# PSUM banks given out by the list scheduler, and a scheduler model with transfer issue time and a shared port: a hybrid conformer and sliding-window layer on eight cores

## What is computed

```python
def reference(x, ...):
    x = x + 0.5 * swiglu_ffn(rmsnorm(x, ffn1_norm), ffn1_w_in, ffn1_w_out)   # hidden width 2816
    h = rmsnorm(x, mix_norm)
    u_conv, q, k, v, g_conv, g_attn = split(h @ w_in)        # 2048, 1024, 256, 256, 1024, 1024
    a = conformer_conv(u_conv, ...)   # GLU, causal depthwise conv of width 31, layer norm, SiLU, projection
    b = sliding_window_gqa(q, k, v, ...)   # 16 q heads, 4 kv heads, window 128, QK norm, T5 bias, sinks
    x = x + (sigmoid(g_conv) * a + sigmoid(g_attn) * b) @ w_out
    return x + 0.5 * swiglu_ffn(rmsnorm(x, ffn2_norm), ffn2_w_in, ffn2_w_out)
```

## Time and profile before

| | us |
|---|---|
| runs of the kernel (median of 3) | 3554.66 (3302.78 to 3849.4) |
| profiled execution: time | 3302.84 |
| profiled execution: span of the slowest core (the profile is of this core) | 3301.1 |
| spans of the eight cores | 3278.3 to 3301.1 |
| TensorE busy (93% of the span) | 3071.1 |
| VectorE, ScalarE, GpSimd busy | 1557.6, 938.3, 779.6 |

### The profile page before, as it was taken

One profiled execution on the slowest core, in us unless ns is written; L12 is line 12 of the kernel. 1 busy time (PEld: TensorE's weight loads), 2 busy tenths in 40 slices (PEclk: granted clock), 3 DMA queues, 4 the chain that ended last, 5 costly groups with the idle time before them and its releaser, 6 DMA issues.

```text
span 3301.1 us, 43930 instructions; the slowest of 8 cores (3278.3 to 3301.1 us)
## 1 busy us (share of the span) xinstructions
PE 3071.1 (93%) x15348; PEld 1402.3 (42%) x15348; DVE 1557.6 (47%) x2374; ACT 938.3 (28%) x1447; POOL 779.6 (24%) x542
## 2 busy tenths in 40 slices
PE   3999999999998999997789999999699999999998
PEld 1444444444443545554333333333244444444444
DVE  5444457544465546364344343344464445533444
ACT  3111135211132232323764444443221112311110
POOL 2100012000012523425165544446200000100000
PEclk9999999999999999998899999999899999999999
DMA  6422236422263432426354334446612223522212
GB/s 166 77 37 38 42 108 167 90 39 39 39 156 114 135 100 85 139 63 175 106 117 141 122 122 122 125 112 213 167 33 38 39 46 104 133 39 39 39 20 102
DMA packets 146772, 312.38 MB, mean 95 GB/s; under 512 B 48896, under 2 KB 57088, under 8 KB 142464
## 3 DMA queue, kind: packets, MB, share of 16 engines
q1 hardware_dynamic: 115744, 221.84, 21.4%
q0 software_dynamic: 30816, 87.74, 16.0%
HBM read 288.19 MB, written 100.66 MB: 118 GB/s over the span
## 4 chain that ended last, share of the span: by engine, by line
PE 79%; DVE 5%; DMA 5%; issue 4%; ACT 3%; SPq 2%; POOL 1%; DVEq 0%; ACTq 0%; POOLq 0%
PE ps L363 79%; SPq L391 2%; DMA xA_45<-x 1%; DVE zfm L618 1%; DVE y L674 1%; DMA xA_43<-x 1%; DMA zsh<-zfm 1%; ACT et_163 L377 0%; DMA xC_182<-x 0%; DMA sg_161<-sig_s 0%; DVE hA_49 L438 0%; POOL toep_92 L643 0%; DVE hA_48 L438 0%; DMA xA_44<-x 0%; POOL toep_90 L643 0%
## 5 line engine op out<-in xcount | busy, mean ns | idle before, releaser
L652 DVE TENSOR_TENSOR y<-ps,cbias 128x512 f32<-128x512 f32 x64 | 43.9, 690 | 185.1 <-PE ps L363 140.5
L377 ACT ACTIVATE tfC_210<-ps 128x512 f32<-128x512 f32 x44 | 26.3, 597 | 311.1 <-PE ps L363 311.1
L377 ACT ACTIVATE tfA_73<-ps 128x512 f32<-128x512 f32 x44 | 26.2, 596 | 286.6 <-PE ps L363 286.5
L377 ACT ACTIVATE et_163<-ps 128x1024 bf16<-128x1024 f32 x63 | 64.3, 1021 | 109.4 <-PE ps L363 108.8
L755 POOL TENSOR_TENSOR pt_166<-et_162,EB 128x1024 bf16<-128x1024 bf16 x31 | 66.3, 2139 | 109.3 <-ACT et_162 L377 109.1
L377 ACT ACTIVATE et_162<-ps 128x1024 bf16<-128x1024 f32 x63 | 64.2, 1018 | 78.1 <-PE ps L363 77.9
L377 ACT ACT_TABLE_LOAD x52 | 66.7, 1283 | 68.1 <-PE ps L363 58.2
L755 POOL TENSOR_TENSOR pt_165<-et_163,EB 128x1024 bf16<-128x1024 bf16 x32 | 68.4, 2138 | 10.8 <-ACT et_163 L377 9.1
L755 POOL TENSOR_TENSOR pt_164<-et_162,EB 128x1024 bf16<-128x1024 bf16 x32 | 68.4, 2138 | 7.9 <-ACT et_162 L377 7.2
L508 DVE SCALAR_TENSOR_TENSOR xA_45<-ps,xA_45 128x512 f32<-128x512 f32 x96 | 64.8, 689 | 11.3 <-PE ps L363 10.6
L508 DVE SCALAR_TENSOR_TENSOR xC_183<-ps,xC_183 128x512 f32<-128x512 f32 x96 | 64.9, 690 | 10.8 <-PE ps L363 9.9
(11 more groups left out here) (747 smaller groups left out, 7440.3 us busy)
## 6 DMA issues: line engine op xcount, KB each, us to landing
zsh<-zfm SPq DMA_DIRECT2D x256, 32.0 KB, 2.0
hM<-h SPq DMA_DIRECT2D x8, 1024.0 KB, 6.9
cact<-cact_s SPq DMA_DIRECT2D x8, 1024.0 KB, 5.8
sig_s<-tfB_124 SPq DMA_DIRECT2D x24, 256.0 KB, 2.3
sig_s<-tfB_125 SPq DMA_DIRECT2D x24, 256.0 KB, 2.3
cact_s<-ct_126 SPq DMA_DIRECT2D x6, 1024.0 KB, 7.2
sg_156<-sig_s SPq DMA_DIRECT2D x22, 256.0 KB, 3.6
sg_157<-sig_s SPq DMA_DIRECT2D x22, 256.0 KB, 4.3
```

Source lines behind the costliest of these rows:

```text
L377: P.add("act", lambda e: e.activation(**kw), reads, writes, 0.21 + n / 1200.0 + (0.3 if accum is not None else 0.0), table=TABLE.get(func))
L652: dve(lambda e, b=b, yv=yv, G=G: e.tensor_tensor(out=yv.ap, in0=ps[:, b, :].rearrange("p (g r c) -> p g r c", g=4, r=8), in1=cbias.t[:, 64 ...
```

## The change

The device work is the same; the bank of each matmul, the order of the queues and the semaphore waits that follow from it are not.

- A bank is now an object (`Bank`) with a list of spots it may take: `ANY` (7 down to 0; SwiGLU, norm and convolution), `MIX` (7 down to 2; q, k, v, the two accumulators, merge, output projection) and `TWO` (the pairs 0, 1 and 2, 3; scores). The first operation that uses it allocates it when the scheduler puts that operation into TensorE's queue. It is given back when its last user has been scheduled, free in model time 0.3 us after the last reader's end.
- `place` looks for spots that no live bank holds and takes the first in the list that is free by then. Projections of q and k are marked `hold`: at most three of them live at once.
- TensorE's step looks at the first 64 ready matmul groups in list order (`SCAN`), asks `place` for each, and takes the first among those that can start earliest (`PATIENCE` 0).
- Model costs: a transfer on SP occupies its queue for 0.64 us up to 64 KB and 0.45 us above (0.1 before). An operation of GpSimd, and one of VectorE with two larger inputs in SBUF (`two`), each wait until the other's is over. Results reach TensorE 0.3 us and other engines 0.12 us after their end (0.2 before). One small GpSimd operation costs 1.7 instead of 0.6.

The diff, cut to its core:

```diff
+SCAN = 64
+PATIENCE = 0.0
+class Bank:
+    def __init__(self, spots, hold=False):
+        self.spots, self.hold = spots, hold
+        self.ops = []
+        self.i = None
...
+    def place(self, o, t):
+        taken, spots = set(), []
+        for b in o.alloc:
+            if b.hold and self.held >= 3:
+                return None, None
+            best = None
+            for sp in b.spots:
+                if any(self.owner[x] is not None or x in taken for x in sp):
+                    continue
+                at = max(self.bfree[x] for x in sp)
+                if best is None or max(at, t) < max(best[0], t):
+                    best = (at, sp)
+            if best is None:
+                return None, None
+            t = max(t, best[0])
+            taken.update(best[1])
+            spots.append(best[1])
+        return t, spots
...
+                if e == "pe":
+                    cand = []
+                    for i in pe_new[:SCAN]:
+                        at, spots = self.place(ops[i], max(free[e], ready[i]))
+                        if at is not None:
+                            cand.append((at, i, spots))
+                    if not cand:
+                        continue
+                    low = min(c[0] for c in cand)
+                    t = low
...
+            if e == "pe":
+                t, pick, spots = next(c for c in cand if c[0] <= low + PATIENCE)
+                pe_new.remove(pick)
+                o = ops[pick]
+                for b, sp in zip(o.alloc, spots):
+                    b.i = sp[0]
+                    b.at = sp
+                    self.held += b.hold
+                    for x in sp:
+                        o.deps.update(self.bprev[x])
+                        self.owner[x] = b
...
+            if o.dma is None and (e == "pool" or o.two):
+                t = max(t, lock["dve" if e == "pool" else "pool"])
+                lock[e] = t + cost
...
+            for b in o.banks:
+                mm_left[b] -= 1
+                if not mm_left[b]:
+                    self.held -= b.hold
+                    for x in b.at:
+                        self.owner[x] = None
+                        self.bfree[x] = max(ops[i].end + (0.3 if ops[i].eng != "pe" else 0.0) for i in b.ops)
+                        self.bprev[x] = b.ops
             for s in succ[pick]:
-                lat = 0.0 if (ops[s].eng == e and o.dma is None) else 0.2
+                lat = 0.0 if (ops[s].eng == e and o.dma is None) else 0.3 if ops[s].eng == "pe" else 0.12
...
+    ANY = [(i,) for i in range(7, -1, -1)]
+    MIX = [(i,) for i in (7, 6, 5, 4, 3, 2)]
+    TWO = [(0, 1), (2, 3)]
...
-        return P.add(eng, fn, reads, writes, 0.1 if q == "sp" else 1.0, dma=key, nbytes=nbytes, after=after)
+        return P.add(eng, fn, reads, writes, (0.64 if nbytes <= 65536 else 0.45) if q == "sp" else 1.0, dma=key, nbytes=nbytes, after=after)
...
-        b = 7
+        b = Bank(ANY)
...
-                ba, bb = banks7.next(), banks7.next()
+                ba, bb = Bank(ANY), Bank(ANY)
...
-    bankB, bankC, bankL = Ring([0, 1, 2, 3, 4]), Ring([5, 6]), Ring([7])
...
-    bankM, bankS, bankV = Ring([0, 1, 2, 3]), Ring([(4, 5)]), Ring([(6, 7)])
...
-            b = bankM.next()
+            b = Bank(MIX, True)
...
-            bo, bd = bankV.next()
+            bo, bd = Bank(MIX), Bank(MIX)
...
-                b0, b1 = bankS.next()
+                sb = Bank(TWO)
```

More of the change, by code:

```diff
@@ L1 @@
+import bisect
 import heapq
@@ L61 @@
 class Op:
-    __slots__ = ("eng", "fn", "deps", "cost", "table", "dma", "nbytes", "start", "end", "pos", "val", "raw", "i")
+    __slots__ = ("eng", "fn", "deps", "cost", "table", "dma", "nbytes", "start", "end", "pos", "val", "raw", "i",
+                 "two", "banks", "alloc")
 class Prog:
@@ L74, in __init__, with add @@
         self.last_dma = {}
-    def add(self, eng, fn, reads, writes, cost, table=None, dma=None, nbytes=0, after=()):
+    def add(self, eng, fn, reads, writes, cost, table=None, dma=None, nbytes=0, after=(), two=False):
         o = Op()
+        o.two, o.banks, o.alloc = two, [], []
         o.i = len(self.ops)
@@ L110, in add @@
             self.last_dma[dma] = o.i
+        for v in list(reads) + list(writes):
+            b = getattr(v, "bank", None)
+            if b is not None and b not in o.banks:
+                o.banks.append(b)
+                if not b.ops:
+                    o.alloc.append(b)
+                b.ops.append(o.i)
         deps.discard(o.i)
@@ L455, in ffn @@
         last = [None]
-        banks7.n = 0 if first else 4
         def load_x(t):
```

175 lines of the change are left out of this document (96 added, 79 removed).

## The result

Two executions of the changed kernel took 3208.29 and 3217.18 us, beside 3300.71 and 3302.78 of the kernel before: a ratio of 0.973, with a 95% interval of 0.967 to 0.979. A second, later measurement gave 0.974 (0.972 to 0.976; 3214.74 and 3216.47 us). The kernel is faster by 2.7%.

The account below looks back on a forecast made before the run. TensorE was taken as the bound, its idle time mostly waits for PSUM banks, which also lower the clock. Bank gains of 71 us, minus 6 for bank choice, plus 5 for costs, gave 70 us: 3233 us, range 3175 to 3320.

Parts of the forecast that it names:

- A: Whole kernel: bank waits were the cause and 60% comes back; 3233 us, own range 3205 to 3265, chance 0.50.
- within: Whole kernel: time not told from no change, about 2% either way, between 3237 and 3369 us; chance 0.48.
- What stays: at nothing, since no edit reaches them: Start (58 us), full SwiGLU slices and second SwiGLU's start (32 us between 2300 and 2400): no gain.
- the loss of 6 for the bank choice: SwiGLU: taking the first free bank in the list, not the longest free, loses slack behind late readers; 6 us.
- Attention, 40 us: Attention, merge, output projection (1700 to 2300 us): three quarters of 54 us of bank waits and their clock come back.
- the announced 25 us: Attention: sign of being right, TensorE's idle time falls from 44 to under 25 us.
- Hand-over and convolution, 19 + 12 by banks and 5 by costs: 1041 to 1700 us: banks gain 19 of 42 us in hand-over, 12 of 22 in convolution; both model edits 5.
- the bound of 10.1 us on both cost edits: Matmuls behind toep: SP issue time and port model together gain between 0 and 10.1 us; half taken.
- The announced signs: Convolution: ct waits go from 12.3 to under 3 us; toep waits halve.
- B: Hand-over and attention: data waits replace bank waits, idle time stays behind pt, sq, toep; 3283 us, chance 0.22.
- C: SwiGLU, norms of late tiles: reusing the latest freed bank makes TensorE wait behind late readers; 3330 us, chance 0.14.
- D: Whole kernel: all bank and toep waits go, with their clock, 128 us; 3175 us, chance 0.14.

Follow-up runs that it names:

- the run with the late start: Changed kernel with the second tile's norm matmul kept ahead of the first tiles' SwiGLU matmuls, which then start near 50 us: 3194.02 us, ratio 0.967.

## Why the prediction failed, and what of it was right

The time was 3208 to 3217 us where 3233 was forecast, inside the range of 3175 to 3320 and inside A's own. A was the mechanism. What failed is the forecast itself: no change beyond 2% was held the likeliest, "within" at 0.48 against "faster" at 0.45, and the kernel is 2.7% faster. The sum of 70 us, 4 us past the bound of 2%, was too small. The step that failed is "What stays: at nothing, since no edit reaches them". On a core at full clock the stages held at nothing gave 32 us of the 44 that were missing, attention 8 more, and the loss of 6 for the bank choice stands in no stage's balance (convolution and hand-over: 2 less than forecast). On the slowest cores themselves (core 5 before, core 7 after: 94 us) attention gave 14 more than forecast and the last stage 12; the first stage's gain went there into the clock of 0.81. Term by term:

- **Attention, 40 us: undersized.** It gave 48 to 51 (644.2 to 596.1 or 592.9; rings put back: 648.1). Three quarters of 54 was too careful: with no engine above 52% beside TensorE, most bank waits went, and their clock with them. Releasers afterwards in the window of the earlier trace rows, in their order:

```profile
PE ps L470 <- POOL mg L893: 12.4, 1, 12.4
PE ps L470 <- DVE xC_181 L607: 4.9, 1, 4.9
PE ps L470 <- DVE tfM_170 L863: 3.8, 4, 1.0
PE ps L470 <- ACT et_163 L478: 2.1, 4, 0.5
```

  The two largest lie behind the last score, which now comes inside the window: mg is the operand of the last tile's output projection, xC belongs to the second SwiGLU. Without them 14.7 of the 32.0 us are left. So by the fixed window the announced 25 us were missed, and up to the last score they were kept; the clock is the announced 0.98, and o and qn are gone from the list.
- **Hand-over and convolution, 19 + 12 by banks and 5 by costs: right in sum (36 against 34), wrong in cause.** Banks alone took 8 where 31 were forecast, since the waits for a bank came back behind the tanh (29.3 us); the costs alone took 29 where 5 were. The failing step there is the bound of 10.1 us on both cost edits, taken from the waits for toep. It priced only what the model says about those instructions. With the costs alone TensorE waits less for qn, too (3.1 us on core 5, 9.9 before). The announced signs came: ct at 1.3 us in the convolution (12.3 before), no wait for toep.

```profile
PE ps L470 <- ACT ct_126 L478: 1.3, 5, 0.4
```

  From 1500 to 1700 us, ct_127 still takes 7.6 us on core 7, and one late zsh 14.6: data, as the prediction had it for a part of that stage.

```profile
PE ps L470 <- DMA zsh<-zfm: 14.6, 1, 14.6
PE ps L470 <- ACT ct_127 L478: 7.6, 6, 2.7
```

- **What stays, at 0: the failed step.** First and last stage gave 21 and 11 us on a core at full clock. "No edit reaches them" was wrong: the rings of SwiGLU and the norm go as well, and an order that changes in the stage behind changes what runs at the seam. The stretch before the first zsh, on core 5 before and after (columns of the earlier trace rows), has lost its idle time:

```profile
940.00:1041.00 101.00, 91.00 (x413) 40.32 (x411) 77.15 (x126) 37.23 (x58) 26.69 (x23) 0.98 0.68 173
```

```profile
940.00:1016.00 76.00, 76.00 (x353) 34.34 (x352) 58.67 (x114) 36.36 (x55) 14.82 (x15) 1.00 0.73 191
```

  Up to 150 us the same core is busy for 105.4 us where it was for 95.0: the early start, of which little is left at the end of the stage, as the run with the late start shows. At the start of the second SwiGLU, TensorE's waits before (2280 to 2420 us, core 5; columns as in the earlier trace rows) and after (2197 to 2337, core 7) are:

```profile
PE ps L363 <- DVE hC_186 L438: 11.2, 1, 11.2
PE ps L363 <- DVE hlC_221 L432: 10.5, 1, 10.5
PE ps L363 <- DVE hC_187 L438: 8.4, 1, 8.4
```

```profile
PE ps L470 <- POOL mg L893: 12.4, 1, 12.4
PE ps L470 <- DVE xC_181 L607: 4.9, 1, 4.9
PE ps L470 <- DVE hidC_193 L595: 2.0, 1, 2.0
```

  Before, the first SwiGLU groups stood ahead of the last tile's output projection in the queue, and TensorE waited three times for a tile's norm. After, the whole output projection comes first; it waits once for its operand mg, and no wait for a norm is left. Which part of the change brings that order stays open, since several runs with banks on demand lose the gain again.

- **Bank choice, 6 us of loss: right in size, wrong in place.** The longest-free choice gains 4 us by the stages and 8 by the time (late start, 3194.02 to 3186.08), and it gains them in the convolution, behind the tanh, not in SwiGLU. There TensorE is idle from 531 to 990 us for 0.9 to 2.1 us on those four cores at full clock, behind hid and x; the 8.1 us are those of core 7, which had been at 0.81.
- **Not foreseen: the clock of 0.81**, 25 us on the slowest cores. It hid about a fifth of the gain. That 3233 lay so near is luck: the sum of 70 us was too small by 44, and this loss was missing.
- **Rivals.** B is out: in attention the idle time went and was not replaced. The Trainium skill's page "TensorE: Matmul & The Clock Gate", section "HAM oscillation — how this bites in real kernels", reports no further gain from PSUM double-buffering in a kernel reworked because its gaps came from transfers; here the gaps came from the banks, and freer banks gave 48 us. C is out in SwiGLU beyond a few us, but its mechanism, a bank taken behind a late reader, is what the banks alone met in the convolution. D's 3175 is near the spans of the cores at full clock (3160 to 3187), and to the best kernel's 3186, but not by D's way: waits for a bank are left (26.7 us of idle time in attention, 15.9 us behind tfB), and the first and last stage make up for them.

## To carry to other kernels

A wait for a PSUM bank on a nearly full TensorE is worth its length and, here, over half as much again in granted clock, and in attention, where the other engines are half idle, most of it came back. A bank given out on demand can also bring a wait, when its last reader is late for reasons of its own: look at who reads the bank before, and what that engine waits for. A planner's cost is no local term: one number that is nearer to the chip moved the queues of the whole stage, so it is priced by the idle time of the whole stage and not by the waits of the instruction that it describes, and leaving it out of the finished kernel does not show its worth, since the other edits cover for it. Before an earlier start is counted, look at when the next tile is ready.

## What the hardware showed that was not expected

- A granted clock of 0.81 on two cores of a die side by side, while the two beside them, as busy, stayed at 1.00: 192 matmuls in 50 us against 233. It lasted 149 to 163 us in the first SwiGLU of six kernels (in one of them on six cores, in one on all eight), all of which begin at 40 to 42 us, and 357 us in one that begins at 48 us; the early start alone, with the issue time as the one change, did not bring it.
- GpSimd's toep took 4.87 us in the mean with the port in the model, 4.78 before, 4.56 with banks on demand and no port model, and 4.55 in the changed kernel (core 5; over 5 us were 7, 5, 2 and 2 of 44). What made the long toep of the earlier trace rows rarer is the order with banks on demand and not the model of the port.
